# Moving 24 row dots past the start of the last matmul stage, and starting the row sums six steps later

## The reference, cut to what matters

```python
a = einsum('chkd,cd->chk', u_tab[eidx], xc)      # 128 dots per token with rows of u
wgt = gelu(a) * g
return einsum('chk,chkd->cd', wgt, v_tab[eidx])  # sum of 128 rows of v per token
```

## Time and profile before

| what | value |
|---|---|
| runs (3) | median 2743.41 us, 2736.26 to 2743.61 |
| profiled execution | 2747.92 us, span 2746.1 us |
| mean granted TensorE clock | 0.956 of full |
| busy, share of the span | PE 91%, DVE 62%, ACT 38%, POOL 15% |
| DMA | 605.95 MB, mean 221 GB/s |

### The profile page before, as it was taken

How to read it: one execution, slowest core, us unless ns; L and a number is a source line. 1 busy time by engine, 2 the same in 40 slices (tenths; PEclk the granted TensorE clock), 3 DMA queues, 4 the chain that set the end, 5 groups by cost and what they waited for, 6 DMA issues and landing times.

```text
span 2746.1 us, 31159 instructions
## 1 busy us (share of the span) xinstructions
PE 2491.8 (91%) x12293; PEld 1900.9 (69%) x12293; DVE 1710.5 (62%) x2974; ACT 1042.2 (38%) x1307; POOL 404.3 (15%) x299
## 2 busy tenths in 40 slices
PE   6998999587877999999989999988988899999996
PEld 4665776333333444677768999988988888888885
DVE  4524334412206547566543998899999488888874
ACT  4844522221104411477233333344554333333332
POOL 0100000000000000000000011133433145444500
PEclk9999999799986999999999999999999999999998
DMA  4433442499991100211022466779999799999972
GB/s 193 180 149 123 179 158 94 161 393 425 425 389 54 61 31 0 92 62 62 31 108 93 153 222 224 270 239 348 343 343 354 292 339 379 376 376 383 375 262 85
DMA packets 159214, 605.95 MB, mean 221 GB/s; under 512 B 13687, under 2 KB 79351, under 8 KB 126360
## 3 DMA queue, kind: packets, MB, share of 16 engines
q1 hardware_dynamic: 91104, 384.32, 37.2%
q0 software_dynamic: 42480, 154.68, 15.3%
q10 hardware_dynamic: 25480, 64.90, 6.2%
HBM read 533.08 MB, written 70.78 MB: 220 GB/s over the span
## 4 chain that ended last, share of the span: by engine, by line
PE 68%; DVE 15%; DMA 10%; issue 4%; ACT 3%; SPq 0%; POOL 0%; ACTq 0%; DVEq 0%; POOLq 0%
PE P L2642 6%; PE P L2644 6%; PE P L2643 6%; DVE window L588 4%; PE P L2538 4%; PE P L2540 4%; PE P L2539 4%; PE P L2194 3%; DMA ug<-in_ur,sparse 3%; PE P L2369 3%; DMA H<-in_w_up 2%; PE P L1997 2%; PE P L1998 2%; PE P L1999 2%; DVE part L588 2%
## 5 line engine op out<-in xcount | busy, mean ns | idle before, releaser
L2538 PE MATMUL P<-hr,part 128*128 128x384 f32 (+1 forms) x1136 | 402.0, 354 | 46.1 <-DVE part L588 45.5
L588 DVE TENSOR_TENSOR part<-raw,part 128x2048 fp32r<-128x2048 f32 x136 | 311.1, 2288 | 191.3 <-ACT part L1852 191.1
L2539 PE MATMUL P<-hr,part 128*128 128x384 f32 (+1 forms) x1136 | 395.1, 348 | 0.0
L2540 PE MATMUL P<-hr,part 128*128 128x384 f32 (+1 forms) x1136 | 394.9, 348 | 0.0
L2657 POOL DMA_INDIRECT ug<-in_ur,sparse x128 | 164.2, 1282 | 1133.0 <-DVE window L1263 758.2
L1852 ACT ACTIVATE part<-raw 128x2048 fp32r<-128x2048 f32 x136 | 260.6, 1916 | 151.1 <-PE P L2644 125.4
L2642 PE MATMUL P<-part,ge 128*128 128x512 f32 x768 | 299.3, 390 | 0.8 <-issue 0.8
L2644 PE MATMUL P<-part,ge 128*128 128x512 f32 x768 | 299.1, 389 | 0.0
L2643 PE MATMUL P<-part,ge 128*128 128x512 f32 x768 | 299.1, 389 | 0.0
L2538 PEld LDWEIGHTS P<-hr,part 128*128 128x128 f32 x1136 | 217.7, 192 | 57.4 <-DVE part L588 51.4
L2539 PEld LDWEIGHTS P<-hr,part 128*128 128x128 f32 x1136 | 217.6, 192 | 5.0
(11 more groups left out here) (359 smaller groups left out, 4525.4 us busy)
## 6 DMA issues: line engine op xcount, KB each, us to landing
raw<-in_u SPq DMA_DIRECT2D x64, 1024.0 KB, 5.0
raw<-in_vd SPq DMA_DIRECT2D x64, 1024.0 KB, 7.8
W<-in_w_up SPq DMA_DIRECT2D x24, 2048.0 KB, 18.7
W<-in_w_in SPq DMA_DIRECT2D x18, 2048.0 KB, 8.5
W<-in_ada_w SPq DMA_DIRECT2D x12, 2048.0 KB, 7.8
a_scratch<-gt ACTq DMA_DIRECT2D x128, 192.0 KB, 3.4
w_scratch<-window ACTq DMA_DIRECT2D x12, 2048.0 KB, 11.3
wr<-w_scratch SPq DMA_DIRECT2D x32, 768.0 KB, 13.1
```

What stands on the lines that cost most here:

```text
L588: return v.tensor_tensor(out=out_, in0=in0, in1=in1, op=op)
L2538: t.matmul(b, wh[:, k, js], HR[0][:, k, lo:S], start=k == 0, stop=False)
L2539: t.matmul(b, wh[:, k, js], HR[1][:, k, lo:S], start=False, stop=False)
L2540: ins = t.matmul(b, wl[:, k, js], HR[0][:, k, lo:S], start=False, stop=k == 7)
```

## The change

The last 24 dots (104 to 127) leave the window stage and go into the first six steps over v, four in each; the dots that stay are strewn at 0.75 per window half. The gelu and `row_weights` (`sw`) move from the end of `ORDER3` to step 6 of `V_STEPS`, and the sums run from step 6: two and three per step, two and four where n is a multiple of 3, so that they end in step 29. Rows 0 to 3 of v are asked for in step 1 and go into the `vg` tiles (the two halves of `VG` change places), rows 4 to 7 at `sw`, into the `UG` tiles.

```diff
-        wg_steps = interleave([("wg", x, i) for x in range(48) for i in range(2)], dots, 0.95) + dots + [("sw",)]
+        late = [dots.pop() for _ in range(24)][::-1]
+        wg_steps = interleave([("wg", x, i) for x in range(48) for i in range(2)], dots, 0.75) + dots
...
             V_STEPS.append(("part", v_unit[n] + 1))
-            V_STEPS += [sums.pop(0) for _ in range(2) if sums]
+            if n in (1, 6):
+                V_STEPS.append(("vr" if n == 1 else "sw", 0))
+            V_STEPS += [late.pop(0) for _ in range(2) if late] or [sums.pop(0) for _ in range(2) if sums]
             if n + 1 < 32:
                 V_STEPS.append(("up", n + 1))
                 V_STEPS.append(("part", v_unit[n] + 2))
-            V_STEPS += [sums.pop(0) for _ in range(3 if n % 4 else 2) if sums]
+            V_STEPS += [late.pop(0) for _ in range(2) if late] or [sums.pop(0) for _ in range(4 if n % 3 == 0 else 3) if sums]
             V_STEPS.append(("down", n))
...
-                    ts(YT[0], VG[0], DOT[:, 0:1], None, MUL).then_inc(s["ys_v"], 1)
+                    ts(YT[0], VG[4], DOT[:, 0:1], None, MUL).then_inc(s["ys_v"], 1)
                 else:
                     dve.wait_ge(s["ys_v"], k)
-                    stt(YT[0], VG[k % 8], DOT[:, k:k + 1], YT[0], MUL, ADD).then_inc(s["ys_v"], 1)
+                    stt(YT[0], VG[(k + 4) % 8], DOT[:, k:k + 1], YT[0], MUL, ADD).then_inc(s["ys_v"], 1)
...
             for kind, n in V_STEPS:
                 if kind == "up":
                     weighted(n)
+                elif kind == "ud":
+                    row_dot(n)
+                elif kind == "sw":
+                    row_weights()
...
             for kind, n in V_STEPS:
                 if kind == "up":
                     first_parts(n)
                 elif kind == "sw":
                     act.wait_ge(s["ud_v"], 128)
                     a.activation(DOT, DOT, ACT.Gelu_apprx_tanh).then_inc(s["hs_a"], 1)
...
             def row_of_v(k):
                 if k < 128:
-                    gp.wait_ge(s["ud_v"], 128)
                     gp.wait_ge(s["ys_v"], k - 7)
                     if k >= 4:
+                        gp.wait_ge(s["ud_v"], 128)
                         gp.wait_ge(s[f"vg{k % 4}"], 16 * (k // 4))
-                    if k % 8 >= 4:
+                    if k % 8 < 4:
                         gp.wait_ge(s["wg_v"], 241)
                         gp.wait_ge(s["wg_mm"], 96)
-                    rows(VG[k % 8], A["v"], EID[:, k:k + 1], s[f"vg{k % 4}"])
+                    rows(VG[(k + 4) % 8], A["v"], EID[:, k:k + 1], s[f"vg{k % 4}"])
...
-                elif kind == "sw":
-                    for k in range(8):
+                elif kind in ("vr", "sw"):
+                    for k in range(4) if kind == "vr" else range(4, 8):
                         row_of_v(k)
```

More of the change, by code:

```diff
@@ L566, in program @@
                 V_STEPS.append(("part", v_unit[n] + 2))
-            V_STEPS += [sums.pop(0) for _ in range(3 if n % 4 else 2) if sums]
+            V_STEPS += [late.pop(0) for _ in range(2) if late] or [sums.pop(0) for _ in range(4 if n % 3 == 0 else 3) if sums]
             V_STEPS.append(("down", n))
+        assert not late
         assert not sums
@@ L1438, in vector_program @@
                     row_dot(*i)
-                elif kind == "sw":
-                    row_weights()
             for kind, n in V_STEPS:
@@ L1952, in scalar_program @@
                     first_parts(*i)
+            for kind, n in V_STEPS:
+                if kind == "up":
+                    first_parts(n)
                 elif kind == "sw":
@@ L1955, in scalar_program @@
                     a.activation(DOT, DOT, ACT.Gelu_apprx_tanh).then_inc(s["hs_a"], 1)
-            for kind, n in V_STEPS:
-                if kind == "up":
-                    first_parts(n)
                 elif kind == "part":
```

## The result

The changed kernel takes **2714.26 us** (median of 4 runs, 2712.28 to 2720.51) against 2741.64 (2736.26 to 2743.61): a ratio of 0.9909, 95% interval 0.9897 to 0.9922. That is 27.4 us less; 20 were forecast. Its profiled execution took 2714.08 us, its span 2712.3. The profiled execution of before was 6 us above its own median, and 6.4 of the 33.8 us between the two spans arose ahead of the window stage, so spans are not compared here, but stages.

What follows compares the result with a forecast made beforehand. DVE bounds the window stage, PE the v stage with almost no room on DVE. Window -27.6 (with -4 and +4), passage -6, v stage +13.5 make -20.1 us: forecast 2723 us, range 2708 to 2740.

Steps and rivals of the forecast that it cites:

- The overrun in the v stage: Steps 6 to 29 of the v stage: sums take DVE past PE's 16.32 us step, 13.5 us of new PE waiting.
- The four `UG` buffers give a dot's row a whole step to arrive: Steps 0 to 5 of the v stage: no wait for the rows of the moved dots.
- the four early gathers: Gathers of v on POOL in step 1: they fill queue space, first use comes later, cost 0.
- the reserve: v stage: the second low part ends 1.75 us before PE needs it, taken off the 15.8 us of DVE overrun.
- The passage: Between window and v stage: without eight gathers and `sw`, 6 us gained of 7.3, bounds 0 and 8.
- The window stage: Loses 24 dots of 1.15 us each on DVE: 27.6 us gained, bounds 18 to 34.
- I take these two as equal, some 4 us each way: Window stage: stalls that no longer hide cost 4 us, fewer waits for gathered rows give 4 us back.
- Transfers binding the v stage: Rival: v stage deliveries fall to 358 GB/s, steps last 18.0 us, 2750 us in all; chance 0.05.
- PE binding the window stage: Rival: PE's 271 us there become 290 and more with half-clock spells, 2736 us in all; chance 0.17.
- The v stage absorbing the sums: Rival: DVE's 12% of room in the v stage is real or the overrun hidden, -34, 2710 us; chance 0.13.
- Waits moved and not work: Rival: the moved dots come out of DVE's waits in the window stage, nothing changes, 2743 us; chance 0.02.
- the rule about 358 GB/s from HBM per core: v stage: by this limit no step could be shorter than 18.0 us; the prediction set it against 376 GB/s held.

Runs made afterwards that it cites:

- v_rows_late: Kernel before, with gelu and row_weights in v step 0, sums from step 1, POOL held before its first eight v gathers until v's first low part: 2728.79 us.
- the dose in between: Changed kernel with its four early gathers of v asked for at the start of the passage instead of in step 1: 2716.56 us.
- small_v: Changed kernel with 60 of the 128 gathers of rows of v replaced by copies of 64 bytes per partition, all sums done: 2717.49 us.
- few_both: Kernel before, with 24 window-stage dots over one column instead of 1024 and their rows replaced by 64 bytes per partition: 2733.84 us.
- even_v: Changed kernel with DVE's work spread evenly: five dots per step in steps 0 to 4, sums from step 5 to step 31: 2710.73 us.
- thin_sums: Changed kernel with the fourth sum in eight v-stage steps over one column instead of 1024, its row still gathered: 2708.14 us.
- after_again: The changed kernel again, unaltered, timed beside a kernel with an even spread on one chip: 2716.02 us.
- even_spread: Changed kernel with five dots per step in steps 0 to 4, sums from step 5, v rows 0 to 3 asked for singly in steps 1 to 4: 2702.84 us.
- sw_in_v: Kernel before, with gelu, row_weights and first eight v gathers listed in v step 0, sums from step 1, POOL not held: 2740.17 us.

## Why the prediction was right, point by point

- **The bound of each stage** was read rightly: DVE in the window stage, PE in the v stage with DVE close behind it. The busy shares hid the second (88% of DVE before, 89% after, one without and one with PE waiting); the timeline of a single step showed it, with the 1.32 us that DVE must wait for ACT counted as taken.
- **The overrun in the v stage** was right in mechanism and nearly in size: 51.04 us for three steps where 50.94 were worked out, and +15.9 in place of +13.5. Of the 2.4 us, 0.9 is the wait at 49 us with what follows it, for which the prediction had written 0 ("The four `UG` buffers give a dot's row a whole step to arrive", and "the four early gathers ... 0"). That step failed: four gathers of v stand before the rows of u, and dot 111 had a lead of 6.7 us, not a step of 16.32. It cost 0.9 to 3.4 us, and 5 where the clock fell. The other 1.5 us: a fourth sum adds 1.38 us to a step and not 1.29, and the reserve absorbed about the first such step (1.6 us), not 2.35.
- **The passage**: forecast 6, bounds 0 and 8, measured 7.9. The cause, eight gathers beside it, is shown by v_rows_late (45.8 us) and by the dose in between. The way was told only in part: the prediction counted bytes beside the chain (13.6 us of transfer), while what shrank most was SP's issue of `gin`, from 7.17 to 0.61 us.
- **The window stage** is the term that was mis-sized, in two places. "24 x 1.15 = 27.6 us": DVE's busy time fell by 24 to 25. And "I take these two as equal, some 4 us each way": they were not equal. Waits for rows went nearly whole (6 to 9 us; the 13.3 that the prediction read hold 3.1 from ahead of the stage), while DVE hardly waited for PE, being idle for 2.7 us in all, and PE's granted clock was 0.99. The term should have been -29 to -35, and the sum -21.5 to -27.5. The two errors point opposite ways, so a part of the closeness of 27.6 to 29 is luck.
- **The rivals.** Transfers binding the v stage: rejected by small_v. PE binding the window stage: PE is at 97% there, but the stage took 279.5 us, not 295. The v stage absorbing the sums: rejected by the seven waits. Waits moved and not work: rejected by DVE's busy time in the window stage, 24 us less. On the rule about 358 GB/s from HBM per core in the Trainium skill ("DMA: Bandwidth & Descriptors", Specifications): the changed kernel moves 381 GB/s over 344 us, so the measurement decides against it for a core alone.

## What to carry to other kernels

When work moves from a stage bound by one engine into a stage bound by another, count the receiving stage by one step of its timeline, forced waits included, not by busy shares: 12% of room here was 0.1 us per step ((3 x 16.55 + 15.26) / 4 = 16.23 against 16.32). Spread what moves so that no step is over; the same work in an even pattern cost the v stage 5 to 6 us and not 16. And for gathers with few buffers ask for the lead of each row, from when its buffer comes free to its use, since here it was the order around them that set it: with fewer bytes in the queues the waits stayed (few_both).

## What the runs showed of the hardware

- Gathers of 0.5 MB beside the passage made one issue on SP take longer, 0.6 to 0.9 us with none, 4.2 with four, 6.4 to 7.2 with eight, and the 1 MB load behind it started 4 to 9 us later. The load itself took 10.1 and 10.3 us with none, 11.0 with four, 11.3 and 15.2 with eight.
- After PE waits of 2.8 and 2.9 us in the v stage (even_v, thin_sums) the granted clock stood at 0.50, that is 1.2 GHz, for 3.4 us, with matmuls 0.43 us apart and not 0.23: 1.6 us more. After waits of 2.6, 3.0 and 3.3 us (after_again, small_v, even_spread) it stayed at 1.00.
- An engine whose list holds no wait runs ahead of its place: in sw_in_v POOL asked for the eight rows of step 0 38 to 58 us before DVE came to that step.
- Gathered rows landed in 10.5 us (median) in the quicker kernel and in 7.6 in the slower: the time to landing by itself tells nothing of whether anyone waits.
